# Moving the second branch's gate projection into the attention task stream, with SiLU made of exp, ln and exp

## The chip, the cores and the metric

The kernel runs on the 8 cores of one Trainium2 chip. Each core takes one of the 8 sequences of the batch and does all four layers on it; the cores exchange nothing. The metric is the device time of the slowest core in microseconds (us).

## What is computed

Each layer normalises its input, projects it once to 9216 columns, and runs two mixers on the projection. Cut to what matters here:

```
h = rmsnorm(x, g_norm[layer]);  proj = h @ w_in[layer]
a_u, a_v, a_gate, q, k, v, b_gate, gate_logits = jnp.split(proj, splits, axis=-1)
y_a = chunked_spatial_gating(gelu(a_u), gelu(a_v), ...) * silu(a_gate)
y_b = dilated_attention(q, k, v) * silu(b_gate)
g_a, g_b = jnp.split(sigmoid(gate_logits), N_BRANCHES, axis=-1)
merged = g_a * (y_a @ w_proj_a[layer]) + g_b * (y_b @ w_proj_b[layer])
x = x + merged @ w_out[layer]
```

A core has 2048 positions and a model width of 1024. The attention has 16 heads of 64 channels and three patterns: keys at distance up to 128 in steps of 1, up to 512 in steps of 4, up to 2048 in steps of 16. The three share one softmax denominator. The part at issue is `silu(b_gate)`: a 1024 by 1024 projection of `h`, x / (1 + exp(-x)) of it, and the product with the attention's output.

## The kernel before, in words

**Layout.** Activations lie transposed, channels on the 128 partitions. `HT` holds the normalised input, `VY` the output of a branch, `M` the merged result, each as 8 channel tiles of 2048 positions in bf16; `XT` is the residual in f32. Since all of them are views of one allocation, the profile calls every SBUF tile "arena" and every PSUM bank "ps". A projection is made of items: one item is 8 matmuls of 128x128 weights against 512 positions into one of the 8 PSUM banks.

**Order.** The program is written as one list per engine (`Prog`). An instruction waits for what it depends on and for nothing else, but each engine runs its list in order, so the order in which the code emits decides what queues behind what. Only TensorE does not wait for its own earlier instructions by semaphore; ScalarE and VectorE do.

**Stages of a layer.** In this order: the V projection with a round trip through a DRAM buffer `vd` (from which keys' values are gathered by stride), the first q and k projections, the attention, the B gate (lines 573 to 586), the merge with `w_pb` (`proj_merge`, L588), the branch A stages, the merge with `w_pa`, and the output projection with the next layer's normalisation.

**Attention.** The heads go in 8 pairs (`hp`). A pair has 4 blocks of 512 queries, and a block has 10 score tasks: 8 of the first two patterns (`s_fn`, L489) and 2 of the third (`s3_fn`, L516; 16 matmuls of 32 columns). A score task computes scores into one bank, ScalarE takes exp of the bank into a `PT` tile, VectorE multiplies it with the mask. Its `pv` function later multiplies the tile with the values, into the block's output banks 0 to 3. For pairs 0 to 6, 8 items of the next pair's q and k projection (`qk_item`, L430) are put between the tasks, one after every fifth; pair 7 has none. After a block's last product, `norm_fn` (L537) takes ln of both denominators and exp of the negative on ScalarE, and two VectorE products write the normalised output to `VY`. At a pair's start `gen_masks` (L458) makes the pair's masks by 6 exps on ScalarE.

**The emission loop (L558 to L571)** walks over all tasks of a layer. At step t it emits task t's score part and then the product part of task t-3:

```
tk["sb"] = 4 + t % 4
tk["pt"] = PT[t % 5]
```

So the score banks 4 to 7 are used in turn by every task, q and k items included, and a task's bank is wanted again four steps later.

**Weights.** `chunks` (L257) lists all weight blocks of 1024x256 in the order of use. Four slots of SBUF hold them; `w_release` issues the DMA for the next block on the POOL queue, and the block waits there until the slot's readers are through. The values are loaded from `vd` on the SP queue by `load_v0` (double buffered), `load_v1` and `load_v2` (single buffers, so each is loaded when the pair before has used it for the last time).

**The B gate stage** runs after the last attention task. It takes 32 items through `proj_fm` (L343); each ends in a Silu on ScalarE (L582) and one VectorE product into `VY` (L583).

Of the kernel before, what the change touches and what calls it, by code (L numbers as in the profile page):

```python
# [174 lines left out]
def build(l0, l1, final):  # L175
# [18 lines left out]
    P = Prog(nc)  # L194
# [63 lines left out]
    for l in range(l0, l1):  # L258
# [3 lines left out]
        for j in range(4):  # L262
            chunks.append(cw(3072, j))
            chunks.append(cw(4096, j))
        for j in range(4):
            chunks.append(cw(6144, j))
        for j in range(4):
            chunks.append(w_pb[l, :, j * WCOLS:(j + 1) * WCOLS])
# [23 lines left out]
    def w_acquire():  # L292
        i = wstate["next_use"]
        wstate["next_use"] = i + 1
        return WS_[i % NSLOT]
# [77 lines left out]
    for l in range(l0, l1):  # L373
# [43 lines left out]
        def load_v1(hp):  # L417
            rk = tuple(("vd", hp, i_) for i_ in range(16))
            P.dma("sp", "vl1", lambda e: e.dma_start(
                out=VL1.ap.rearrange("p (r b) c -> p r b c", r=4),  # L420
                in_=vd[:, hp, :].rearrange("(b p r) c -> p r b c", b=4, p=128, r=4)), reads=rk, writes=VL1.k())
# [8 lines left out]
        def qk_item(hp, which, s, qb=7):  # L430
# [10 lines left out]
            if (hp % 2 == 1) and which == 1 and s == 3:  # L441
                w_release()
                w_release()

        items = [(w, s) for s in range(4) for w in range(2)]
        for ii, (w, s) in enumerate(items):
            qk_item(0, w, s, ii)
# [6 lines left out]
        for hp in range(8):  # L454
# [94 lines left out]
            if hp + 1 < 8:  # L549
                for ii, (w_, s_) in reversed(list(enumerate(items))):  # L550
                    ptasks.insert(5 * ii + 5, dict(
                        s=lambda tk, hp=hp, w_=w_, s_=s_: qk_item(hp + 1, w_, s_, tk["sb"]),
                        pv=lambda tk: None, before=[], after=[]))
                ptasks[9]["after"].append(lambda hp=hp: load_v0(hp + 1))
                ptasks[-1]["after"].append(lambda hp=hp: load_v1(hp + 1))
            tasks += ptasks

        SKEW = 3  # L558
# [12 lines left out]
                    f()  # L571

        ti = [0]
        for j in range(4):
            wsl = w_acquire()
            for f2 in range(2):
                hp = 2 * j + f2

                def ev(s, bank, hp=hp):
                    t1 = T1[ti[0] % 4]  # L580
                    ti[0] += 1
                    act(t1.ap, PS[bank][:, :], AF.Silu, psk(bank), t1.k())  # L582
                    tt(VY.ap[:, hp, s * 512:(s + 1) * 512], VY.ap[:, hp, s * 512:(s + 1) * 512], t1.ap, ALU.mult,  # L583
                       VY.k2(hp, s * 512, (s + 1) * 512) + t1.k(), VY.k2(hp, s * 512, (s + 1) * 512))
                proj_fm(wsl, f2 * 128, next_banks(), ev)
            w_release()

        def proj_merge(accumulate):  # L588
            for j in range(4):
# [235 lines left out]
```

How the kernel before makes its waits and increments, by code:

```python
            def run(e, eng):  # L111
                for ins in self.ins[e]:
                    for src, val in ins["waits"]:
                        v = cnts[src[1]][val] if src[0] == "e" else val
                        eng.wait_ge(sems[src], v)
                    r = ins["fn"](eng)
                    if ins["dma"] is not None:
                        r.then_inc(sems[("d", ins["dma"])], 16)
                    elif ins["signal"]:
                        r.then_inc(sems[("e", e)], 1)
                if e == "sp":
                    for g in final_waits:
                        eng.wait_ge(sems[("d", g)], self.groups[g])
```

## Time and profile before

| | |
|---|---|
| median of the 2 runs shown | 4704.23 us (4436.76 and 4971.7) |
| time of the profiled execution | 4439.41 us |
| span of its slowest core, core 2 | 4437.8 us |
| spans of the other cores | 4403.8 to 4431.1 us |
| TensorE busy | 4182.8 us, 94% of the span, 31168 matmuls |
| VectorE busy | 1815.1 us, 41% |
| ScalarE busy | 1746.9 us, 39% |
| chain of waits that ended last | TensorE 86%, ScalarE 5%, DMA 5%, issue 2%, VectorE 2% |
| ScalarE table loads | 29, of 1283 ns |
| mean granted TensorE clock of the core | 0.940 |

Times in the profile are us from the start of the span of core 2 unless marked ns. PE is TensorE's matmuls, PEld its weight loads, DVE is VectorE, ACT is ScalarE, POOL and SP are the queues that issue DMAs. L241, L246, L252 and L255 are the lines of the helpers for a matmul, an activation, a product or sum of two tensors, and a copy. The granted clock is 1.00 at 2.4 GHz and 0.50 at 1.2 GHz; a mean between the two is a stretch that had both.

### The profile page before, as it was taken

The page shows a single profiled execution, that of the slowest core. Times are in us where ns is not written, and L with a number is a line of the kernel's source. Part 1 is how long each engine was busy: PE and PEld are TensorE (multiplying, and loading weights), DVE is VectorE, ACT ScalarE, POOL GpSimd, SP SyncE. Part 2 cuts the span into 40 slices and gives each one's busy share as a digit, 9 for nine tenths or more (in the row PEclk, how much of TensorE's full clock was granted, in tenths as well). Part 3 has the DMA queues.
Part 4 walks back from the last instruction along what each step waited for, and adds up shares of the span by engine and source line. Part 5 has one row for each costly group of instructions (what it writes and reads, how often), then busy time and mean ns, then how long its engine had stood idle before and what let it go on. Part 6 is the DMA issues. An engine that isn't in the chain of part 4 may idle for free.

```text
span 4437.8 us, 84096 instructions; the slowest of 8 cores (4403.8 to 4437.8 us)
## 1 busy us (share of the span) xinstructions
PE 4182.8 (94%) x31168; PEld 2447.0 (55%) x31168; DVE 1815.1 (41%) x3285; ACT 1746.9 (39%) x3085; POOL 170.3 (4%) x200
## 2 busy tenths in 40 slices
PE   5999999899899999999989999999999999999997
PEld 3666654644566665554466666464446666646444
DVE  3344432353444442244434444224443444323435
ACT  3355541421245553242225555233222555524213
POOL 0000000000000000000000000000000000000000
PEclk7999979999999988999999997999999999799999
DMA  4522212322342221222252221223224222122222
GB/s 123 106 52 53 51 27 34 43 34 39 70 86 54 54 47 20 39 39 38 29 111 53 54 53 40 29 29 48 39 34 110 54 54 54 30 34 38 34 34 86
DMA packets 426842, 227.99 MB, mean 51 GB/s; under 512 B 204368, under 2 KB 421840, under 8 KB 426448
## 3 DMA queue, kind: packets, MB, share of 16 engines
q0 software_dynamic: 199808, 100.68, 18.0%
q1 hardware_dynamic: 226640, 121.93, 9.6%
q8 instruction: 262, 4.29, 0.4%
q14 instruction: 132, 1.08, 0.1%
HBM read 289.71 MB, written 33.55 MB: 73 GB/s over the span
## 4 chain that ended last, share of the span: by engine, by line
PE 86%; ACT 5%; DMA 5%; issue 2%; DVE 2%; ACTq 0%; DVEq 0%; SPq 0%; POOL 0%; POOLq 0%
PE ps L241 85%; ACT arena L246 5%; DMA arena<-vd 2%; DVE arena L252 1%; DMA arena<-w_in 1%; DMA arena<-x 1%; DVE arena L356 0%; PE ps L317 0%; DMA out<-arena 0%; PE ps L759 0%; PE ps L383 0%; DVE arena L338 0%; DVE arena L255 0%; DVE arena L361 0%; ACTq L115 0%
## 5 line engine op out<-in xcount | busy, mean ns | idle before, releaser
L241 PE MATMUL ps<-arena 128*128 128x512 bf16 (+5 forms) x30880 | 4134.3, 297 | 182.8 <-DVE arena L252 70.6
L241 PEld LDWEIGHTS ps<-arena 128*128 128x128 bf16 (+1 forms) x30880 | 2407.5, 111 | 1908.7 <-issue 591.0
L246 ACT ACTIVATE arena<-ps 128x512 bf16<-128x512 f32 (+2 forms) x2400 | 1388.8, 595 | 2352.0 <-PE ps L241 2054.2
L252 DVE TENSOR_TENSOR arena<-arena 128x512 bf16<-128x512 bf16 (+1 forms) x1600 | 710.4, 457 | 895.8 <-ACT arena L246 869.2
L252 DVE TENSOR_TENSOR arena<-ps,arena 128x512 bf16<-128x512 f32 (+3 forms) x800 | 529.1, 673 | 1059.9 <-PE ps L241 816.6
L255 DVE CAST arena<-ps 128x512 bf16<-128x512 f32 x320 | 221.4, 692 | 388.8 <-PE ps L241 385.5
L246 ACT ACTIVATE arena<-arena 128x512 bf16<-128x512 f32 (+4 forms) x528 | 262.9, 528 | 249.5 <-DVE arena L252 105.1
L289 POOL DMA_DIRECT2D arena<-w_in x144 | 126.3, 878 | 3009.0 <-PE ps L241 2991.8
L697 DVE SCALAR_TENSOR_TENSOR arena<-arena,ps 128x512 bf16<-128x512 bf16 x128 | 88.1, 688 | 92.0 <-ACT arena L246 92.0
L356 DVE SCALAR_TENSOR_TENSOR arena<-arena 128x512 bf16<-128x512 f32 x128 | 86.2, 746 | 28.6 <-ACT arena L246 28.6
L700 DVE SCALAR_TENSOR_TENSOR arena<-arena 128x512 bf16<-128x512 bf16 x128 | 88.6, 692 | 13.7 <-DVE arena L697 0.5
L248 ACT ACTIVATE arena<-arena 128x1024 bf16<-128x1024 f32 x64 | 67.7, 1057 | 6.1
L246 ACT ACT_TABLE_LOAD x29 | 37.2, 1283 | 73.9 <-PE ps L241 49.0
L317 PE MATMUL ps<-arena 128*128 128x128 f32 x128 | 24.0, 343 | 25.3 <-DMA arena<-x 22.2
L338 DVE TENSOR_SCALAR arena<-ps 128x512 f32<-128x512 f32 x20 | 13.8, 692 | 71.4 <-PE ps L241 71.4
L255 DVE COPY arena<-ps 128x512 f32<-128x512 f32 x32 | 22.0, 691 | 42.7 <-PE ps L317 36.8
L383 PE MATMUL ps<-arena 128*128 128x128 f32 x32 | 9.9, 401 | 28.9 <-DVE arena L252 27.5
L317 PEld LDWEIGHTS ps<-arena 128*128 128x128 f32 x128 | 18.7, 177 | 30.2 <-issue 30.1
L289 POOL DMA_DIRECT2D arena<-w_pb x16 | 14.0, 874 | 545.7 <-PE ps L241 545.7
L655 DVE TENSOR_SCALAR arena<-arena 128x1024 bf16<-128x1024 bf16 x64 | 28.6, 483 | 11.4 <-ACT arena L246 8.0
L289 POOL DMA_DIRECT2D arena<-w_pa x16 | 14.0, 873 | 400.6 <-PE ps L241 400.6
L361 DVE SCALAR_TENSOR_TENSOR arena<-arena 128x512 f32<-128x512 f32 x32 | 21.6, 746 | 7.8 <-ACT arena L246 7.8
(14 smaller groups left out, 72.8 us busy)
## 6 DMA issues: line engine op xcount, KB each, us to landing
arena<-w_in POOLq DMA_DIRECT2D x144, 512.0 KB, 7.0
arena<-vd SPq DMA_DIRECT2D x96, 768.0 KB, 7.2
vd<-arena SPq DMA_DIRECT2D x128, 192.0 KB, 1.9
arena<-x SPq DMA_DIRECT2D x16, 512.0 KB, 14.3
arena<-w_pb POOLq DMA_DIRECT2D x16, 512.0 KB, 5.9
arena<-w_pa POOLq DMA_DIRECT2D x16, 512.0 KB, 5.8
arena<-w_o POOLq DMA_DIRECT2D x16, 512.0 KB, 7.0
out<-arena SPq DMA_DIRECT2D x16, 512.0 KB, 7.8
```

The lines of the kernel that those rows point to most:

```text
L241: P.op("pe", lambda e: e.matmul(out, lhsT=lhsT, rhs=rhs, start=start, stop=stop, skip_group_check=True), reads, writes)
L246: P.op("act", lambda e: e.activation(out=out, in_=in_, func=func, scale=scale), reads, writes)
L248: P.op("act", lambda e: e.activation(out=out, in_=in_, func=func, scale=scale, accum_out=accum_out), reads, writes)
L252: P.op(eng, lambda e: e.tensor_tensor(out=out, in0=in0, in1=in1, op=op), reads, writes)
L255: P.op(eng, lambda e: e.tensor_copy(out=out, in_=in_), reads, writes)
L289: P.dma("pool", "w%d" % (i % NSLOT), lambda e: e.dma_start(out=slot.ap, in_=src), reads=(), writes=slot.k())
L317: P.op("pe", lambda e, bank=bank, c4=c4, xs=xs, ct=ct: e.transpose(PS[bank][:, c4 * 128:(c4 + 1) * 128], xs.ap[:, ct * 128:(ct + 1) * 128] ...
L356: P.op("dve", lambda e, ct=ct, rs=rs: e.scalar_tensor_tensor(out=HT.ap[:, ct, s * 512:(s + 1) * 512], in0=XT.ap[:, ct, s * 512:(s + 1) * 512],
L361: P.op("dve", lambda e, ct=ct, rs=rs: e.scalar_tensor_tensor(out=XT.ap[:, ct, s * 512:(s + 1) * 512], in0=XT.ap[:, ct, s * 512:(s + 1) * 512],
L655: P.op("dve", lambda e, c=c: e.tensor_scalar(out=VN[:, :, c, :], in0=VN[:, :, c, :], scalar1=SSQ.ap[:, c:c + 1], scalar2=None, op0=ALU.mul ...
L697: P.op("dve", lambda e, sgt=sgt, s=s: e.scalar_tensor_tensor(out=sgt.ap, in0=sgt.ap, scalar=1.0, in1=PS[gbk[s]][:, :], op0=ALU.add, op1=AL ...
L700: P.op("dve", lambda e, sgt=sgt, uus=uus: e.scalar_tensor_tensor(out=uus, in0=uus, scalar=0.5, in1=sgt.ap, op0=ALU.mult, op1=ALU.mult), uu ...
```

## The change

It drops the B gate stage. Its 32 items become `bg_item`s: those of pairs 0 to 6 are tasks in the attention stream of the pair that follows, 4 in each of the pairs 1 to 7, at place 3 of each quarter of the pair's task list; the 4 of pair 7 come after the stream, in banks 0 to 3. Silu is replaced by exp, ln(1 + .), exp(- .), so sigmoid comes out, and a VectorE product with the bank. The gate weights move forward in `chunks`: each j now has its q, k and gate block in a row.

```diff
         for j in range(4):
             chunks.append(cw(3072, j))
             chunks.append(cw(4096, j))
-        for j in range(4):
             chunks.append(cw(6144, j))
...
+        bg_slots = {}
+
+        def bg_item(p, sp_, qb, tl):
+            j = p // 2
+            if j not in bg_slots:
+                bg_slots[j] = w_acquire()
+            wsl = bg_slots[j]
+            c0 = (p % 2) * 128
+            for ct in range(8):
+                mm(PS[qb][:, :], wsl.ap[:, ct, c0:c0 + 128], HT.ap[:, ct, sp_ * 512:(sp_ + 1) * 512],
+                   ct == 0, ct == 7, wsl.k2(ct) + HT.k2(ct, sp_ * 512, (sp_ + 1) * 512), psk(qb))
+            act(tl.ap, PS[qb][:, :], AF.Exp, psk(qb), tl.k(), scale=-1.0)
+            P.op("act", lambda e: e.activation(out=tl.ap, in_=tl.ap, func=AF.Ln, bias=1.0), tl.k(), tl.k())
+            act(tl.ap, tl.ap, AF.Exp, tl.k(), tl.k(), scale=-1.0)
+            tt(tl.ap, PS[qb][:, :], tl.ap, ALU.mult, psk(qb) + tl.k(), tl.k())
+            yk = VY.k2(p, sp_ * 512, (sp_ + 1) * 512)
+            tt(VY.ap[:, p, sp_ * 512:(sp_ + 1) * 512], VY.ap[:, p, sp_ * 512:(sp_ + 1) * 512], tl.ap, ALU.mult,
+               yk + tl.k(), yk)
+            if (p % 2 == 1) and sp_ == 3:
+                w_release()
...
+            if hp >= 1:
+                per = len(ptasks) // 4
+                for b_ in reversed(range(4)):
+                    ptasks.insert(per * b_ + 3, dict(
+                        s=lambda tk, hp=hp, b_=b_: bg_item(hp - 1, b_, tk["sb"], tk["pt"]),
+                        pv=lambda tk: None, before=[], after=[]))
...
-        for j in range(4):
-            wsl = w_acquire()
-            for f2 in range(2):
-                hp = 2 * j + f2
-
-                def ev(s, bank, hp=hp):
-                    t1 = T1[ti[0] % 4]
-                    ti[0] += 1
-                    act(t1.ap, PS[bank][:, :], AF.Silu, psk(bank), t1.k())
-                    tt(VY.ap[:, hp, s * 512:(s + 1) * 512], VY.ap[:, hp, s * 512:(s + 1) * 512], t1.ap, ALU.mult,
-                       VY.k2(hp, s * 512, (s + 1) * 512) + t1.k(), VY.k2(hp, s * 512, (s + 1) * 512))
-                proj_fm(wsl, f2 * 128, next_banks(), ev)
-            w_release()
+        for s_ in range(4):
+            bg_item(7, s_, s_, T1[s_])
```

## Rows read from the trace of the kernel before

**Rows 1.** Windows: length, busy (count) by engine, clock, DMA; layer 0's attention, gate
```profile
162.10:609.30 447.20, 420.80 (x4386) 279.40 (x4386) 212.80 (x439) 247.84 (x456) 7.00 (x8) 0.90 0.24 52
609.30:664.60 55.30, 55.30 (x259) 25.09 (x257) 14.57 (x33) 20.97 (x35) 2.62 (x3) 1.00 0.23 29
```

**Rows 2.** Windows of the B gate stage of all four layers, the sum
```profile
sum 221.50, PE 221.50 PEld 100.37 DVE 58.25 ACT 84.15 POOL 10.48; mean PE 55.38 PEld 25.09 DVE 14.56 ACT 21.04 POOL 2.62
```

**Rows 3.** Windows of layer 0's attention: pair 1, pair 4, and pairs 1 to 6
```profile
215.50:273.20 57.70, 52.94 (x558) 34.76 (x557) 27.30 (x57) 31.84 (x61) 0.87 (x1) 0.94 0.25 56
385.80:438.40 52.60, 50.56 (x558) 33.49 (x558) 27.37 (x57) 30.63 (x56) 0.87 (x1) 1.00 0.23 50
215.50:551.30 335.80, 314.88 (x3338) 206.70 (x3338) 163.97 (x337) 187.60 (x349) 5.24 (x6) 0.95 0.25 53
```

**Rows 4.** Windows of pair 7: layer 0, a stretch inside it, four layers' sum
```profile
551.30:609.30 58.00, 54.87 (x502) 39.26 (x502) 22.38 (x49) 31.40 (x56) 0.89 (x1) 0.56 0.17 32
...
561.00:605.00 44.00, 43.74 (x400) 30.70 (x401) 16.55 (x36) 22.79 (x39) 0.00 (x0) 0.50 0.01 1
...
sum 231.40, PE 219.51 PEld 157.10 DVE 89.57 ACT 124.74 POOL 3.51; mean PE 54.88 PEld 39.27 DVE 22.39 ACT 31.18 POOL 0.88
```

**Rows 5.** TensorE's waits (us, times, longest): layer 0's attention, then layer 3's
```profile
PE ps L241 <- DVE arena L252: 18.9, 30, 2.0
PE ps L241 <- DMA arena<-vd: 7.0, 4, 2.8
...
PE ps L241 <- DVE arena L252: 17.4, 31, 2.0
PE ps L241 <- DMA arena<-vd: 0.9, 1, 0.9
```

**Rows 6.** TensorE's waits in layer 0: pairs 1 to 6, then pair 7
```profile
PE ps L241 <- DVE arena L252: 15.1, 25, 2.0
PE ps L241 <- DMA arena<-vd: 5.8, 3, 2.8
...
PE ps L241 <- DVE arena L252: 1.9, 1, 1.9
PE ps L241 <- DMA arena<-vd: 1.2, 1, 1.2
```

**Rows 7.** Timeline (start, length, engine, line) around one block's end, layer 0, pair 2
```profile
286.44 2.55 ACT L246 ACTIVATE arena<-ps 128x512 bf16<-128x512 f32 x4 [2.05 <-PE ps L241]
...
289.08 0.63 ACT L246 ACTIVATE arena<-arena 128x512 f32<-128x512 f32 x1
289.62 1.55 ACT L246 ACTIVATE arena<-ps 128x512 bf16<-128x512 f32 x3
289.88 1.48 DVE L252 TENSOR_TENSOR arena<-ps,arena 64x512 bf16<-64x512 f32 x2 [1.66 <-ACT arena L246]
291.38 1.10 DVE L252 TENSOR_TENSOR arena<-arena 128x512 bf16<-128x512 bf16 x3
...
291.95 0.72 PE L241 MATMUL ps<-arena 128*128 128x128 bf16 x6 [0.53 <-DVE arena L252]
```

**Rows 8.** Groups (busy, mean ns, idle before) in layer 0's B gate stage
```profile
L246 ACT ACTIVATE arena<-ps 128x512 bf16<-128x512 f32 x31 | 18.4, 597 | 32.8 <-PE ps L241 32.8
L252 DVE TENSOR_TENSOR arena<-arena 128x512 bf16<-128x512 bf16 x31 | 13.2, 425 | 38.6 <-ACT arena L246 38.6
```

**Rows 9.** Timeline of TensorE at the start of pair 7, layer 0
```profile
550.73 4.63 PE L241 MATMUL ps<-arena 128*128 128x128 bf16 x50
557.30 2.77 PE L241 MATMUL ps<-arena 128*128 128x128 bf16 x30 [1.95 <-DVE arena L252]
561.26 2.08 PE L241 MATMUL ps<-arena 128*128 128x128 bf16 x19 [1.19 <-DMA arena<-vd]
```

**Rows 10.** Timeline of ScalarE, layer 0: the first table load since the attention began
```profile
611.35 1.28 ACT L246 ACT_TABLE_LOAD   x1 [0.40 <-PE ps L241]
```

**Rows 11.** The page's DMA issues: count, size, median us to landing
```profile
arena<-vd SPq DMA_DIRECT2D x96, 768.0 KB, 7.2
```

## The prediction

> **What bounds the kernel now.** I read the table of engines and the chain of waits first: TensorE is busy in 94% of the span and carries 86% of the chain, so what counts is what happens to TensorE's time. The windows by stage come next. The B gate stage of a layer is 55.3 us in which TensorE is never idle and the clock is 1.00 [rows 1]; in four layers it is 221.5 us [rows 2]. The attention is 447.2 us in layer 0, of which TensorE is idle for 26.4, at a mean clock of 0.90 [rows 1]. So the stage that goes away has no slack in it, and the one that takes its work in has two kinds: idle time of TensorE, and time at the lower clock.
>
> Idle time: TensorE waits 18.9 us for VectorE and 7.0 us for the values' DMA in layer 0's attention, 17.4 and 0.9 in layer 3's [rows 5]; pairs 1 to 6 of layer 0 have 15.1 and 5.8 of it [rows 6]. Clock: pair 4, all of it at 1.00, takes 52.6 us, pair 1, at 0.94, takes 57.7 [rows 3]. Pair 7 has no q and k items, yet takes 58.0 us at 0.56, and 44 us of it lie wholly at 0.50, the 1.2 GHz level [rows 4]. The timeline shows what came before the fall: an idle 1.95 us behind the masks' VectorE work and 1.19 us for the values' DMA, within 6 us [rows 9]. The clock then stays low through narrow matmuls of 32 and 128 columns, and is back as soon as the gate stage's 512-column matmuls begin (1.00 in the second of rows 1).
>
> **What an item costs on TensorE.** The gate stage is 32 items in 55.3 us, 1.73 us each [rows 1]. All 128 are still done. If nothing else happened, the change would move 221.5 us and save nothing: the gain must come from slack.
>
> **Gate stage out, tail in.** Out go 55.4 us per layer [rows 2]. Four items remain after the stream: 6.9 us. The last two use banks 2 and 3, which the last block's normalisation still reads: in [rows 7] that takes from about 287.7 (two of the four in the first row are its ln) to 291.36, 3.7 us, and the first two items cover 3.5. I take 7.3 us. The merge does not wait for them: its product matmuls for a block of positions need only that block's item, and those for the last block come seven groups of 8 matmuls, 12 us, after the last item, against about 3 us of chain behind it. The Silu table load falls away (1.28 us [rows 10]); it ran on ScalarE while TensorE worked, so it is worth nothing. Exp and Ln alternate all through the attention with no table load before that one [rows 10], so the new ln adds none.
>
> **24 items in pairs 1 to 6.** They add 24 x 1.73 = 41.5 us of TensorE work. Does their ScalarE and VectorE work make TensorE wait? An item needs exp from the bank 0.60 [rows 8], ln and exp in SBUF about 0.63 each (the row of 0.63 [rows 7]), then a product with the bank at about 0.74 (half of the 1.48 [rows 7]) and one in SBUF at 0.43 [rows 8]. The old stage had one of 0.60 and one of 0.43. On average there is room: pair 4 has ScalarE busy 30.6 of 52.6 us and VectorE 27.4 [rows 3]; with four items each they come to 38 and 32 of about 59.
>
> But the items land at the worst place, just behind a block's normalisation. I walk through it from the end of the last block's products (287.5). Now: ScalarE does ln, ln, exp until 289.7, then three exps back to back until 291.2; VectorE's two normalising products end at 291.36, the mask product behind them at 291.8, and TensorE starts at 291.95 after 0.53 idle [rows 7]. With the item two tasks after the block's start: TensorE has 1.73 us more to do, ScalarE does the next task's exp until 290.2 and then the item's three until 292.2, and the exps of the two tasks behind it end at about 292.7 and 293.2. VectorE frees the item's bank near 293.1, finishes the item near 293.6, and has the next two masks at 294.0 and 294.5. On TensorE the item, three tasks' matmuls and a q or k item lie ahead of the task that wants the bank: it gets there at about 294.1, and to the first of these masks at 294.5. Nothing waits, and the old 0.53 us is gone, since the item lies in front of it. So in these pairs the item covers most of the waits for VectorE. It covers most of the DMA waits too, because it stands between the issue of `load_v1` and its first use: with 1.73 us more in between, a wait of at most 2.8 us [rows 6] is at most 1.1.
>
> Of the 20.9 us of idle in pairs 1 to 6 of layer 0 [rows 6], less in layer 3 (18.3 in all pairs [rows 5]), I take 18.5 as the mean and let 80% go: -15. The weight loads shift: three instead of two come near the end of pairs 2, 4 and 6, on the POOL queue, where each waits for its slot's readers only. Every block is issued ten tasks or more ahead of its use, and nothing but weights is queued behind it there. Their cost is that they share the DMA engines with the values' loads (7.2 us to landing [rows 11]); at worst the DMA waits double, +5.8, at best nothing.
>
> **The clock.** Price of the lower level: pair 4 without its 8 items is 52.6 - 13.8 = 38.8 us at 1.00; pair 7, the same tasks, is 58.0 at 0.56. So 19.2 us for 88% of 58 us at the low level, 0.38 us per us. Pairs 1 to 6 have a mean of 0.95 [rows 3], 33 us at 0.50 per layer, worth 12.6 us. The lower level follows idle stretches there, and these shrink; I let half of it come back: -6. Pairs 1 to 6 then add 41.5 - 15 - 6 = 20.5 us. Bounds: 41.5 - 18.5 - 12.6 = 10.4, and, with no slack filled and 0.6 us of new wait per item (one ScalarE instruction), 56.
>
> **Pair 7.** The first of its items stands ahead of both waits of [rows 9], so the clock should not fall there. Warm throughout, it would be 38.8 + 6.9 = 45.7 us. Between its items it has ten tasks and no q or k item, so there ScalarE's chain is not covered as above: the bank is wanted some 0.8 us too early in each block, +3 against some 2 saved. I take it that the clock falls in about a third of the pair, +6, and get 53: -5 against 58. Bounds: warm -11; cold as now, with 6.9 us of items that at 0.50 take twice as long, +12 after the waits they cover.
>
> **Sum per layer:** -55.4 + 7.3 + 20.5 - 5 = -32.6 us, 130 in four layers. Against the profiled execution's 4439.4 that is **4309 us**. That execution is at the level of the lower of the two runs shown (4436.8), not at their median of 4704; the forecast is for executions like it. All at the good end: -55.4 + 7.3 + 10.4 - 11 = -48.7, 4245 us. All at the bad: -55.4 + 7.3 + 56 + 12 = +20, 4519 us.
>
> **Rivals.**
> *Clock stays low in pair 7.* The items come every ten tasks; after each the narrow matmuls return, and [rows 4] show that these alone never brought the clock back in 44 us. Then pair 7 costs +12 instead of -5: 4309 + 4 x 17 = 4377, -1.4%. Against it: in pairs 1 to 6 the same tasks hold a mean of 0.95 with one wide item per five. The Trainium skill, page "TensorE: Matmul & The Clock Gate", section "A second HAM failure mode: psum-queue depth-cycling", speaks for this rival: cycling through PSUM banks lets TensorE idle briefly between groups, often enough that the clock swings between its levels. These tasks cycle through four banks; taken for pair 7 alone the rule gives this rival's time, and its row, 0.56, agrees. Chance 0.17.
>
> *All slack is filled.* Pairs 1 to 7 at 1.00 and without waits: 4245. For it: pair 4 holds 1.00 already. Chance 0.15.
>
> *Slower: the item's chain holds its score bank.* Place: ScalarE, three instructions in a row that wait for each other, and behind them the exps of the next tasks. Price: 0.60 + 0.63 + 0.63 + 0.74 and about 0.25 of semaphores, 2.85 us per item, all of it idle on TensorE for 112 items, with no slack filled: 4439 - 4 x 48.1 + 112 x 1.73 + 319 = 4760. It decides from about 2 us of new wait per item, (130 + 89) / 112; that is 4528. For it: ScalarE already runs without a break through 4.7 us here [rows 7]. Against it: 4.5 us of TensorE work lie between the item and the next user of its bank. Chance 0.07.
>
> **Chances and range.** The forecast's own case has 0.61, with 4270 to 4350 about it. About 2% (89 us) is what a measurement tells from no change, so faster means under 4350: 0.15 of the full gain and 0.55 of the forecast's case, 0.70. Within 2%: the clock rival and the forecast's slow edge, 0.22. Slower: 0.08. The range runs from a little below the full gain to a little above the clock rival with doubled DMA waits (4377 + 4 x 5.8 = 4400): 4235 to 4425.
>
> **What would show it.** Right: after the last attention task only some 7 us of 512-column matmuls before the merge; pairs 1 to 6 at some 356 us in layer 0, waits for VectorE near 3 us; pair 7 near 53 us with a clock of 0.75 or more; 25 table loads. Wrong: waits of TensorE for VectorE of over 1 us right after the items; pair 7 at a clock near 0.6; table loads inside the attention; longer waits for the values' DMA at the starts of pairs 3, 5 and 7.

## The result and the profile after

The changed kernel takes 0.9927 of the time before, interval 0.9910 to 0.9943: some 32 us less, where 130 were forecast. The interval lies clear of 1, but the change is below the 2% that the prediction had called the least that a measurement tells from none. Its executions took 4401.6 to 4415.8 us beside 4436.8 to 4441.2 of the kernel before; the one profiled took 4407.62, against 4439.41. (The higher of the two times shown before, 4971.7, is of a disturbed execution, as some of either kernel are; they are left out.)

The page of the changed kernel: span, busy time of the engines, the chain that ended last, table loads, the values' DMA.

```profile
span 4406.0 us, 84976 instructions; the slowest of 8 cores (4366.7 to 4406.0 us)
...
PE 4190.4 (95%) x31168; PEld 2446.8 (56%) x31168; DVE 1899.9 (43%) x3413; ACT 1886.8 (43%) x3337; POOL 170.3 (4%) x200
...
PE 79%; ACT 8%; DMA 5%; issue 4%; DVE 4%; SPq 0%; ACTq 0%; DVEq 0%; POOL 0%; POOLq 0%
...
L246 ACT ACT_TABLE_LOAD x25 | 32.1, 1283 | 66.5 <-PE ps L241 43.2
...
arena<-vd SPq DMA_DIRECT2D x96, 768.0 KB, 7.9
```

ScalarE and VectorE have more to do, and ScalarE has 8% of the chain where it had 5; TensorE's busy time is hardly changed (4182.8 before), and its busy share is a point higher. What is to be explained is busy time, not waits. The windows of core 2 (the first line of before, the others of after), columns as in [rows 1]: the sum of pairs 1 to 6 over four layers before; then layer 0's pairs 1 to 6, their sum over four layers, pair 1 alone, pair 7 of layer 0 and its sum, the sum of the four items that come behind the stream.

```profile
sum 1335.10, PE 1261.11 PEld 825.18 DVE 656.16 ACT 750.18 POOL 20.98; mean PE 315.28 PEld 206.30 DVE 164.04 ACT 187.55 POOL 5.25
...
213.90:578.40 364.50, 356.74 (x3530) 226.01 (x3529) 190.46 (x385) 228.78 (x421) 7.87 (x9) 0.99 0.26 53
...
sum 1461.80, PE 1433.34 PEld 906.94 DVE 761.18 ACT 915.60 POOL 31.49; mean PE 358.33 PEld 226.73 DVE 190.30 ACT 228.90 POOL 7.87
...
213.90:273.70 59.80, 58.65 (x590) 37.40 (x590) 31.76 (x65) 38.12 (x71) 0.87 (x1) 1.00 0.24 53
...
578.40:645.30 66.90, 63.68 (x533) 41.68 (x533) 26.41 (x57) 37.86 (x68) 0.87 (x1) 0.64 0.16 31
...
sum 262.50, PE 247.36 PEld 162.26 DVE 105.52 ACT 151.33 POOL 3.49; mean PE 61.84 PEld 40.56 DVE 26.38 ACT 37.83 POOL 0.87
...
sum 27.80, PE 27.80 PEld 12.77 DVE 12.60 ACT 24.05 POOL 0.00; mean PE 6.95 PEld 3.19 DVE 3.15 ACT 6.01 POOL 0.00
```

Per layer, the mean of four on core 2, the answer to [rows 1 to 4]:

| part | forecast | measured | from |
|---|---|---|---|
| gate stage out, four items behind the stream | -48.1 | -48.4 | (27.80 - 221.50) / 4 |
| pairs 1 to 6 | +20.5 | +31.7 | (1461.80 - 1335.10) / 4 |
| pair 7 | -5 | +7.8 | (262.50 - 231.40) / 4 |
| rest of the layer | 0 | about +1 | what is left of the sum |
| sum | -32.6 | -8 | 32 us in four layers |

TensorE's waits in layer 0 (us, times, longest), first pairs 1 to 6, then pair 7, against [rows 6]:

```profile
PE ps L241 <- DVE arena L252: 5.6, 22, 0.6
PE ps L241 <- DMA arena<-vd: 1.8, 2, 1.1
...
PE ps L241 <- DVE arena L252: 2.0, 3, 1.4
PE ps L241 <- ACT arena L246: 0.8, 2, 0.6
```

In pairs 1 to 6 the waits fell by 13.5 us, from 20.9 to 7.4, and the clock rose from 0.95 to 0.99. Both slacks that the forecast counted on were used. Yet pair 1 at a full clock takes 59.8 us, and pair 4 of before, at a full clock too, took 52.6 [rows 3]: 7.2 us more for 6.9 us of items. TensorE's busy time alone rose by more, from 50.56 to 58.65 us, 8.1 for 6.9. Something new ate what the waits gave.

**Where it went** shows around the block's end of [rows 7]. First TensorE before, then after, each from its own timeline (start, length):

```profile
287.45 0.41 PE L241 MATMUL ps<-arena 64*128 64x128 bf16 x8
```
```profile
289.01 0.33 PE L241 MATMUL ps<-arena 64*128 64x128 bf16 x3
...
291.33 0.39 PE L241 MATMUL ps<-arena 64*128 64x128 bf16 x4
...
288.95 4.26 PE L241 MATMUL ps<-arena 64*128 64x128 bf16 x40
293.73 4.49 PE L241 MATMUL ps<-arena 128*128 128x128 bf16 x44 [0.51 <-DVE arena L252]
```

The four score matmuls of one task use 64 rows of the array: head 0's operands lie on partitions 0 to 63, head 1's on 64 to 127. The q or k item has no product part, so three steps after it no product stands between the scores of two tasks. These are a task of head 0 and one of head 1, and before the change their eight matmuls took 0.41 us together. Afterwards the new item and a product stand between them: four in 0.39 us, and four more in about as much, 2.3 us later. The Trainium skill, page "TensorE: Matmul & The Clock Gate", section "Part 3: Packing small matmuls — row/col tiling", says that matmuls on different row groups of the array run concurrently. The trace agrees, with eight in 0.41 us beside four in 0.39.

Taken over all the fully warm stretches of pairs 1 to 6 as medians from start to start (my own matching of the matmul records to the order of emission), the two score steps behind a block's normalisation went from 122 and 218 ns to 327 and 327: +0.31 us. The step of the third pattern behind them went from 1.17 to 1.39, +0.22, which is a wait; the 0.51 in the last row above is one of these, a long one. The q or k item that had covered the normalisation went from 2.37 to 1.82, -0.55. The two losses together eat the gain, and the item's own 1.74 us come on top.

The wait is there because the product follows its score at a distance of three *steps*, and an item is a step. The rows of ScalarE and VectorE for this stretch, same columns:

```profile
290.86 0.63 ACT L246 ACTIVATE arena<-arena 128x512 f32<-128x512 f32 x1
291.39 1.06 ACT L246 ACTIVATE arena<-ps 128x512 bf16<-128x512 f32 x2
292.55 0.63 ACT L456 ACTIVATE arena<-arena 128x512 bf16<-128x512 bf16 x1
293.27 0.63 ACT L246 ACTIVATE arena<-arena 128x512 bf16<-128x512 bf16 x1
```
```profile
291.66 1.48 DVE L252 TENSOR_TENSOR arena<-ps,arena 64x512 bf16<-64x512 f32 x2 [1.66 <-ACT arena L246]
293.15 0.43 DVE L252 TENSOR_TENSOR arena<-arena 128x512 bf16<-128x512 bf16 x1
294.01 0.69 DVE L252 TENSOR_TENSOR arena<-ps,arena 128x512 bf16<-128x512 f32 x1 [0.42 <-ACT arena L246]
```

VectorE ends the two normalising products at 293.14, and the mask product that TensorE waits for at 293.58. Before the change, the three steps between the block's third score and its product were the fourth score task, the third pattern's and the q or k item, and the product stood behind that item. Now they are the new item, the fourth task and the third pattern's, and the q or k item comes behind the product. So TensorE has one item and two tasks in between, as before: the new item stands in the other's place and adds no distance.

### The profile page after: what moved, and what is told of

Its sections match the earlier page's. It is cut to its first block, busy times and chain, and to the rows that moved or that the text cites. A ratio compares the mean times of both kernels' runs of the same rounds, so it can differ in the third digit from the quotient of the medians.

```text
span 4406.0 us, 84976 instructions; the slowest of 8 cores (4366.7 to 4406.0 us)
## 1 busy us (share of the span) xinstructions
PE 4190.4 (95%) x31168; PEld 2446.8 (56%) x31168; DVE 1899.9 (43%) x3413; ACT 1886.8 (43%) x3337; POOL 170.3 (4%) x200
## 4 chain that ended last, share of the span: by engine, by line
PE 79%; ACT 8%; DMA 5%; issue 4%; DVE 4%; SPq 0%; ACTq 0%; DVEq 0%; POOL 0%; POOLq 0%
PE ps L241 78%; ACT arena L246 8%; DVE arena L252 3%; DMA arena<-vd 2%; DMA arena<-w_in 1%; DMA arena<-x 1%; DVE arena L355 0%; DMA arena<-w_o 0%; ACTq L115 0%; PE ps L774 0%; DVEq L115 0%; DMA out<-arena 0%; SPq L424 0%; PE ps L382 0%; DVE arena L337 0%
## 5 line engine op out<-in xcount | busy, mean ns | idle before, releaser
L252 DVE TENSOR_TENSOR arena<-ps,arena 128x512 bf16<-128x512 f32 (+3 forms) x928 | 618.0, 676 | 1140.7 <-PE ps L241 829.5
L246 ACT ACTIVATE arena<-arena 128x512 bf16<-128x512 f32 (+4 forms) x656 | 343.7, 548 | 267.8 <-DVE arena L252 104.9
L456 ACT ACTIVATE arena<-arena 128x512 bf16<-128x512 bf16 x128 | 80.8, 631 | 12.6 <-ACT arena L246 1.1
L316 PE MATMUL ps<-arena 128*128 128x128 f32 x128 | 23.8, 342 | 23.9 <-DMA arena<-x 22.7
L337 DVE TENSOR_SCALAR arena<-ps 128x512 f32<-128x512 f32 x20 | 13.8, 692 | 70.5 <-PE ps L241 70.5
L316 PEld LDWEIGHTS ps<-arena 128*128 128x128 f32 x128 | 18.5, 176 | 28.9 <-issue 28.7
```

Source lines behind the costliest of these rows:

```text
L246: P.op("act", lambda e: e.activation(out=out, in_=in_, func=func, scale=scale), reads, writes)
L252: P.op(eng, lambda e: e.tensor_tensor(out=out, in0=in0, in1=in1, op=op), reads, writes)
L316: P.op("pe", lambda e, bank=bank, c4=c4, xs=xs, ct=ct: e.transpose(PS[bank][:, c4 * 128:(c4 + 1) * 128], xs.ap[:, ct * 128:(ct + 1) * 128] ...
L456: P.op("act", lambda e: e.activation(out=tl.ap, in_=tl.ap, func=AF.Ln, bias=1.0), tl.k(), tl.k())
```

## The experiments

All ratios are to the kernel before, with their intervals; where there is none, times of executions stand beside those of the kernels named. The table gives the mean of four layers on core 1, for which the records could be matched to the emitted matmuls one by one in every kernel: time, TensorE's idle time, clock. Core 1 is a little shorter than core 2 (before: 331.6 against 333.8 us in pairs 1 to 6).

| kernel | ratio | pairs 1 to 6 | pair 7 |
|---|---|---|---|
| before | 1 | 331.6, 18.1, 0.96 | 57.4, 2.7, 0.54 |
| after | 0.9927 | 362.8, 6.5, 0.99 | 63.3, 2.7, 0.71 |
| e1_place4 | 0.9862 | 360.3, 23.8, 0.98 | 62.3, 3.6, 0.73 |
| e5_one_act | 0.9852 | 362.1, 5.9, 0.99 | 56.2, 1.1, 0.79 |
| e6_place4_one_act | 0.9826 | 360.2, 24.0, 0.98 | 54.0, 3.1, 0.85 |
| e11_skew4 | - | 358.0, 1.1, 0.96 | 67.1, 5.6, 0.69 |
| e8_eight_in_7 | - | 354.9, 21.8, 0.98 | 68.7, 5.8, 0.84 |
| e4_eight_in_7 | 1.0083 | 354.9, 7.1, 0.99 | 68.2, 5.1, 0.84 |
| e2_wide7 | 0.9989 | 331.6, 17.9, 0.96 | 57.4, 4.0, 0.96 |
| e3_head_order | 1.0236 | 347.5, 15.8, 0.94 | 60.3, 4.9, 0.55 |
| e7_head_pairs | 0.9528 | 295.3, 8.1, 0.93 | 43.6, 5.1, 0.76 |
| e9_pairs_gate | - | 342.8, 16.8, 0.96 | 60.8, 12.5, 0.78 |
| e13_pairs_gate2 | 0.9779 | 356.9, 23.1, 0.92 | 60.9, 13.3, 0.78 |
| e14, the same, one act | 0.9672 | 346.5, 19.9, 0.95 | 56.2, 11.3, 0.81 |
| e10_pairs_eight_in_7 | - | 336.7, 15.1, 0.95 | 59.6, 6.8, 0.89 |
| e12_pairs_only_7 | - | 296.4, 8.1, 0.93 | 61.1, 6.8, 0.86 |
| e15_pairs_wide7 | 0.957 | 297.3, 7.2, 0.92 | 48.2, 1.8, 0.96 |

### The item one place later

```diff
-                    ptasks.insert(per * b_ + 3, dict(
+                    ptasks.insert(per * b_ + 4, dict(
```

> The changed kernel with each moved item one place later (place 4 of its quarter instead of 3), nothing else. Theory P (overlap of two heads): where a q or k item leaves a hole in the products, two score tasks follow each other on TensorE, one on partitions 0 to 63 and one on 64 to 127, and run at the same time (the start-to-start step of the first is 122 ns in the kernel before, 327 ns in the changed one, where the item stands between the two). One place later the item leaves these two together and gives another two the same chance: 0.3 to 0.6 us less per item in pairs 1 to 6, 96 items, so 30 to 58 us below the changed kernel, about 4350 to 4375. Theory C (ScalarE's chain of three): the item is only one task further from the normalisation; at most the 0.23 us of wait at the third-pattern task goes, 0 to 22 us less, 4385 to 4408.

Measured: 0.9862 [0.9814, 0.9909]. The two score steps behind the normalisation are back at 122 and some 220 ns, and a second such pair has come up (224 and 356), since the new item has no product part either. But the steps behind them grew, the third pattern's to 1.81 us and another to 0.68. In layer 0 the waits of pairs 1 to 6 show it; the second row is one of these waits.

```profile
PE ps L241 <- DVE arena L252: 20.2, 39, 1.0
...
298.16 4.07 PE L241 MATMUL ps<-arena 128*128 128x128 bf16 x48 [0.92 <-DVE arena L252]
```

So the overlap is real and one place away, and it is largely traded for waits: 17.3 us more idle time per layer than after, yet 2.5 us less in all (table). The executions took 4377.8 to 4397.1 us, on average 19 under the changed kernel's, where the overlap theory had 30 to 58.

### Two of the three ScalarE operations left out

```diff
-            P.op("act", lambda e: e.activation(out=tl.ap, in_=tl.ap, func=AF.Ln, bias=1.0), tl.k(), tl.k())
-            act(tl.ap, tl.ap, AF.Exp, tl.k(), tl.k(), scale=-1.0)
```

> The changed kernel with the item's ln and second exp left out (one ScalarE instruction per item instead of three; the gate's values are then not sigmoid). Theory C (the chain of three is what ate the gain): without it the wait of 0.23 us at the third-pattern task goes in 96 blocks, 21 us, and the waits of pair 7 shrink: 20 to 45 us below the changed kernel, 4362 to 4387. If the broken overlap of two heads is the larger part (theory P), the steps of 327 ns behind the block's start stay as they are and the kernel stays above 4360. If the chain were all of it, the kernel would come near my forecast of 4309.

> Place 4 and one ScalarE instruction per item (ln and second exp left out). In the place-4 kernel the overlaps are back (122 and 224 ns), but the step of the third-pattern task has grown from 1170 to 1814 ns and one score step from 356 to 678. Theory C+P (both costs are real, and place 4 trades one for the other): both steps go back, 0.9 us in 96 blocks, 70 to 100 us below the place-4 kernel, 4290 to 4320. Rival (these steps wait for TensorE's own order, not for ScalarE): no change from 4388.

Measured: e5, at place 3, 0.9852 [0.9837, 0.9867]; e6, at place 4, 0.9826 [0.9804, 0.9847]. In pairs 1 to 6 nothing moved: 362.1 beside 362.8, and 360.2 beside 360.3; the third pattern's step stays at 1.39 and 1.81 us. So the waits there do not come from the item's ScalarE chain, which is what e6 was to find out; what is left is the normalisation, whose ScalarE and VectorE work stands ahead of the mask product, as in the rows above (read from the rows; no run changed that order). The forecast for e6 (some 70 to 100 us under place 4) was missed by far; it came out about 20 under it. All of the gain lies in pair 7. There four layers of e5 read, on core 2:

```profile
sum 230.10, PE 220.64 PEld 149.31 DVE 106.56 ACT 132.64 POOL 3.50; mean PE 55.16 PEld 37.33 DVE 26.64 ACT 33.16 POOL 0.87
```

That is 57.5 us per layer against 65.6 after: the chain costs 8.1 us per layer in pair 7 (7.1 on core 1) and nothing in pairs 1 to 6. Only 1.4 us of the 8.1 are idle time of TensorE (3.8 against 2.4 us); 6.7 are busy time, and go with a clock of 0.68 against 0.78. In pair 7 no q or k item stands beside the chain.

### A distance of four steps

```diff
-        SKEW = 3
+        SKEW = 4
```

> The changed kernel with the product part four steps behind the score part instead of three, nothing else. Theory S (the wait behind the normalisation was never covered by the item, because the distance between a score task and its product is counted in steps, and the item takes one of them): one more step is 0.7 to 1.7 us more for every mask, the waits at the third-pattern task (0.23 us in 96 blocks) and most of pair 7's (3.8 us per layer) go, 20 to 50 us below the changed kernel, 4355 to 4385. Rival (those waits come from an engine that is simply full): within 10 us of 4406.

Measured: 4382.1 to 4394.8 us, 18 under the changed kernel on average, where 20 to 50 were expected. The waits for VectorE in layer 0's pairs 1 to 6 are gone (0.2 us in one wait, beside 5.6), but the pairs fell by 4.8 us only, with the clock at 0.96 instead of 0.99, and pair 7 got longer (67.1), with twice the idle time (5.6). So the distance in steps was what left the wait: a pair that is at the full clock throughout takes 57.4 us where it takes 59.4 in the changed kernel. Why the clock is lower is open.

### What the overlap is worth

The kernel before, all tasks of head 0 in a block ahead of those of head 1:

```diff
-                for wi in range(0, 8, 2):
-                    for hh in range(2):
+                for hh in range(2):
+                    for wi in range(0, 8, 2):
```

> The kernel before, with the score tasks of a block ordered all of the first head, then all of the second, so that neighbours use the same half of the partitions. Theory P (overlap of two heads): the quick steps of 122 and 218 ns become about 330 each, 0.3 us per hole and two holes per block, 0.6 us for 28 x 4 blocks and less where a wait covers it: the kernel is 30 to 75 us slower than before. Rival (the quick steps come from weight loads that ran ahead during the wait before them): nothing changes, within 10 us.

The kernel before, with the scores of two heads issued together and the two products behind them; the q and k items moved between such pairs of tasks:

```diff
+            n = 2 if (t + 1 < len(tasks) and tasks[t].get("head") == 0
+                      and tasks[t + 1].get("head") == 1) else 1
+            for u in range(t, t + n):
...
+                    tk["s"](tk)
+            for u in range(t, t + n):
...
+                    tk["pv"](tk)
...
-                    ptasks.insert(5 * ii + 5, dict(
+                    ptasks.insert(10 * (ii // 2) + (4, 10)[ii % 2], dict(
```

> The kernel before, where the two heads' score tasks of the same work are emitted one right after the other, then the two products; the q and k items stand between such pairs and the two third-pattern tasks are neighbours. Theory P: eight more pairs of score tasks per head pair overlap, 0.31 us each, and four pairs of third-pattern tasks, some 0.5 us each: 4 to 5 us per head pair, 32 of them, less what turns into waits for ScalarE: 50 to 150 us faster than before. Rival (the overlap needs the preceding wait, which lets the queue fill): within 15 us of before.

Measured: e3 is slower, 1.0236 [1.0193, 1.028]. It is +105 us, where 30 to 75 were expected. With the same head on both sides of the missing product the eight matmuls no longer run side by side: by medians as above, the eight score steps of a full block of the first two patterns take 3.38 us instead of 2.71, 0.34 us per q or k item, which would be 76 us over 224 items. The rest goes with a lower clock (0.94 against 0.96 in pairs 1 to 6 on core 1) and a pair 7 that is 2.9 us longer though it has no such item; why is open. e7, which lets every pair of tasks overlap, is the fastest kernel of this study: **0.9528 [0.9512, 0.9543]**, 4230 to 4240 us. It has the B gate stage as before. Its page (span and engines), layer 0's pairs 1 to 6, and pair 7's sum:

```profile
span 4238.1 us, 84320 instructions; the slowest of 8 cores (4205.6 to 4238.1 us)
...
PE 4008.5 (95%) x31168; PEld 2402.0 (57%) x31168; DVE 1803.7 (43%) x3285; ACT 1727.1 (41%) x3085; POOL 170.3 (4%) x200
...
210.70:514.70 304.00, 291.17 (x3339) 203.10 (x3340) 161.93 (x337) 184.93 (x349) 5.24 (x6) 0.92 0.28 59
...
sum 176.90, PE 154.76 PEld 124.78 DVE 87.39 ACT 114.54 POOL 3.50; mean PE 38.69 PEld 31.20 DVE 21.85 ACT 28.64 POOL 0.88
```

TensorE's busy time fell by 174 us with the same 31168 matmuls. "95% busy" had hidden an array with half of its rows unused.

### The studied change on top of it

e9 and e13 put the gate items into e7's stream, between pairs of tasks; e9 at attention place 8 of each block, e13 with the first of a pair at place 2. In e9, and in e10 further down, the gate, q and k blocks are used in another order than they were loaded in, so they are exchanged; the work is the same. In e13 and e14 they are used in the order of loading. e14 leaves ln and the second exp out. The cut is e13's; e9 has `10 * b_ + 8` for every block.

```diff
+                    more.append((10 * b_ + 8 if b_ else 2, dict(
+                        s=lambda tk, hp=hp, b_=b_: bg_item(hp - 1, b_, tk["sb"], tk["pt"]),
```

> The head-pair kernel (4238) with the studied change on top: the gate items with exp, ln, exp in the stream, one per block in pairs 1 to 7, each between two pairs of score tasks and away from the normalisation. If the idle and the low clock that an item can fill are what the change is worth, and no overlap of heads is broken: the stage of 55.4 goes, each item costs 1.73 us less what it fills; pairs 1 to 6 have 1.6 us of idle and a clock of 0.92 in the head-pair kernel, so 1.5 to 3 us each come back, 10 to 18 per layer, and pair 7 0 to 5: 4165 to 4200. If the chain of three costs TensorE more in this denser stream (theory C): 4220 to 4260.

> The head-pair kernel with the studied change on top, the first gate item of a pair ahead of its first q item so that gate, q and k weight blocks are used in the order of loading; items at places 2, 18, 28 and 38 of the 40 tasks, each between two pairs of tasks. If overlaps kept are all that was missing: 1.5 to 3 us per pair of idle and low clock come back, 4165 to 4205. If the chain of three ScalarE instructions costs as much here as in pair 7 of the run with two items per block there: 4235 to 4280, no better than the head-pair kernel's 4238.

> The same with the item's ln and second exp left out. Theory C: 25 to 60 us below the run before, near 4200. If the chain is covered in pairs 1 to 6 and costs in pair 7 alone: 10 to 30 us below.

Measured: e9 4278.8 to 4282.9 us; e13 0.9779 [0.9748, 0.981], 4334 to 4346 us; e14 0.9672 [0.963, 0.9714], 4279 to 4293. Both e9 and e13 had been expected at 4165 to 4205 by the theory I favoured, at 4220 to 4280 by the other, and are above both. They are slower than e7 without the change, e9 by some 48 us, e13 by about 107. Layer 0 of e13, pairs 1 to 6, and TensorE's waits there:

```profile
210.00:570.70 360.70, 336.81 (x3531) 220.18 (x3531) 183.37 (x383) 224.44 (x414) 7.87 (x9) 0.92 0.25 51
```
```profile
PE ps L241 <- ACT arena L246: 10.6, 6, 2.3
...
PE ps L241 <- DMA arena<-vd: 7.3, 2, 4.2
...
PE ps L241 <- DVE arena L252: 4.7, 17, 0.5
```

Against e7 on core 1, 41.5 us of items cost 61.6 in pairs 1 to 6, and 6.9 cost 17.3 in pair 7: +31 us per layer after the 48 that the stage gives back (by the ratios 111 us in all). Most of it is idle time, 15.0 us more in pairs 1 to 6 and 8.2 in pair 7 (table). In pairs 1 to 6 of all four layers (core 2) the waits for ScalarE all come in a pair's first block, behind the item at place 2. In layer 0's pair 2, ScalarE has the pair's six mask exps there (first row), then exps of scores, the normalisation's, the item's three; TensorE waits for it at the third pattern's task (second row).

```profile
267.28 2.14 ACT L246 ACTIVATE arena<-arena 128x256 bf16<-128x256 f32 x6 [1.11 <-DVE arena L252]
```
```profile
275.38 0.82 PE L241 MATMUL ps<-arena 64*128 64x32 bf16 x10 [2.26 <-ACT arena L246]
```

e14, without two thirds of the chain, is 10.4 us per layer shorter in pairs 1 to 6 and 4.7 in pair 7, some 50 us in all. But e9 has the full chain and is a little faster still. It differs from e13 in one place per pair, 8 instead of 2 (and by it in the exchanged blocks), and in layer 0's pairs 1 to 6 it has no wait for ScalarE:

```profile
PE ps L241 <- DVE arena L252: 13.7, 13, 2.2
PE ps L241 <- DMA arena<-vd: 3.6, 2, 1.9
```

So on this order the chain costs pairs 1 to 6 time where the item stands beside the mask exps, not everywhere, and neither the better place nor a shorter chain brings the change down to e7; the two together were not tried. In the odd pairs of e13 and e14 stand 24 us of waits for the values' DMA (four layers, core 2); e7 has 15 of them already. The weights' DMA adds 5.5 us there in e13 and 11.2 in e14. The cause of what was added is open.

### Pair 7: clock, chain or items

e2 is the kernel before, with eight items in pair 7 whose result nobody uses (8 matmuls of 512 columns each, no evictions). e15 is the same on e7. Both do that work in addition.

```diff
+                def wide(tk):
+                    for ct in range(8):
+                        mm(PS[tk["sb"]][:, :], WS_[0].ap[:, ct, 0:128], HT.ap[:, ct, 0:512], ...)
```

> The kernel before, with 8 useless items of 8 matmuls of 512 columns put into pair 7, one after every fifth task, their results unread. Theory W (pair 7 is slow for want of wide matmuls: the clock falls at its start and narrow matmuls do not bring it back): pair 7 takes about 52 to 55 us instead of 58 although it does 13.8 us more, with a clock over 0.9; the kernel is 12 to 24 us faster than before. Rival (the clock follows the waits, not the kind of matmul): pair 7 stays near 0.56 and takes at least 58 + 13.8 us; the kernel is 55 us or more slower.

> The head-pair kernel with 8 useless items of 8 wide matmuls in pair 7, no ScalarE or VectorE work with them. The same kernel with 8 true items there had pair 7 at 61.9 us with a clock of 0.86 and 7.9 us of idle. If the chain is what holds pair 7: 49 to 52 us, clock over 0.93, idle under 3 us, though the kernel as a whole is then 20 to 32 us slower than the head-pair kernel (the work is extra). If it is the clock's own behaviour between sparse items: above 58 us.

e4 and e8 keep four gate items in each of the pairs 1 to 5 and put the last eight into pair 7. e8 has them where the q and k items would be and the others at place 4; e4 has them two tasks earlier (`5 * ii + 3`), not behind every fifth task as its expectation says, and issues three weight loads per layer too few, so that blocks come late and are not the right ones. The cut is e8's. e10 is the same on e7's order. e12 is e7 with eight true gate items in pair 7 and 24 left in the stage.

```diff
+            if hp == 7:
+                for ii in reversed(range(8)):
+                    ptasks.insert(5 * ii + 5, dict(
+                        s=lambda tk, ii=ii: bg_item(5 + ii // 4, ii % 4, tk["sb"], tk["pt"]),
```

> The changed kernel with pair 7 hosting 8 items (those of pairs 5 and 6) after every fifth task, and pair 6 none; pairs 1 to 5 as in the changed kernel. Theory W (wide matmuls hold the clock of pair 7): pair 7 takes 53 to 56 us with 8 items where it now takes 65.6 with 4, its clock is over 0.9, pair 6 goes back to about 53.5 from 61; in all 60 to 85 us below the changed kernel, 4320 to 4345. Rival (waits at the start of the pair hold the clock down): pair 7 near 72 us and no gain over the changed kernel beyond 5 us.

> Items of pairs 5 and 6 in pair 7 (8, after every fifth task), none in pair 6, the others at place 4. The useless-item run had pair 7 at 57.5 us with a clock of 0.94 (57.8 and 0.55 before). Theory W: pair 7 at 58 to 62 us with a clock over 0.85, pair 6 at about 54; 25 to 45 us below the place-4 kernel. Theory C: eight chains of three in 57 us make TensorE wait for ScalarE and the clock falls again, pair 7 at 66 us or more and nothing gained over place 4.

> As the run before, but pair 7 hosts 8 items (of pairs 5 and 6) and pair 6 none. Pair 7 of the place-4 kernel with 8 such items took 68.7 us with waits for the chain, the one with 8 useless items 57.5 us. With the heads in pairs I expect 54 to 58 us for pair 7 if the chain costs little, 60 or more if it is what holds it; in all within 25 us of the run before, faster if the clock counts more, slower if the chain does.

> The head-pair kernel with only pair 7 hosting items: 8 of them (pairs 0 and 1), with exp, ln, exp; the other 24 stay in the stage of their own with Silu. Pair 7 has 44.3 us at a clock of 0.78 and 6.2 us of idle without items. Theory W: it comes to 50 to 54 us with 8 items of 1.73 us, so 4 to 8 us per layer are gained, 4205 to 4222. Theory C: the chain makes it 58 us or more, nothing gained or a loss, 4235 to 4255.

Measured: e2 0.9989 [0.9964, 1.0013]; e15 0.957 [0.9542, 0.9598]; e4 1.0083 [1.0049, 1.0117]; e8 4381.6 and 4388.3 us; e10 4258 to 4269; e12 4245.0 and 4247.2. Of these, e8 came out level with place 4 (4377.8 to 4397.1) and e12 at 4235 to 4255, both as the chain theory had it; e10 is some 17 us under e9. e4 had been expected 60 to 85 us under the changed kernel and is some 78 above it: not by the attention, which is no longer (table), but by waits for weights, 131 us on core 1 against 37. I had expected e2 to win 12 to 24 us. It wins nothing, and loses nothing with 13.8 us of useless work in each pair 7. Pair 7's sums over four layers on core 2, first e2, then e15, then e12:

```profile
sum 230.60, PE 215.68 PEld 142.44 DVE 88.96 ACT 119.37 POOL 3.50; mean PE 53.92 PEld 35.61 DVE 22.24 ACT 29.84 POOL 0.88
```
```profile
sum 193.80, PE 187.18 PEld 132.44 DVE 90.39 ACT 117.46 POOL 3.50; mean PE 46.80 PEld 33.11 DVE 22.60 ACT 29.37 POOL 0.88
```
```profile
sum 244.20, PE 216.71 PEld 148.78 DVE 115.84 ACT 168.48 POOL 5.80; mean PE 54.18 PEld 37.20 DVE 28.96 ACT 42.12 POOL 1.45
```

Three things follow. **The price of the clock:** before, pair 7 took 57.85 us at 0.55; e2 has 57.65 at 0.94 and 13.8 us of it are the added items. So e2 does the same tasks in 57.65 - 13.8 = 43.85 us, 14.0 less. Not all of that is the clock's. A useless item has no product part either, so twice in a block two tasks of different heads come to run side by side in e2, which they never do in pair 7 of before:

```profile
567.41 0.41 PE L241 MATMUL ps<-arena 64*128 64x128 bf16 x8
```

With 0.31 us or more for each of the seven full ones, that is at least 2 us (an estimate), and leaves some 11 to 12 for the low clock, not the 19.2 of the prediction. That had taken pair 4 without its items as its measure, which has the side-by-side tasks that pair 7 lacks, and is among the shortest pairs; pair 1 takes over 5 us more [rows 3]. **The items hold the clock** with no evictions behind them: 0.94 and 0.96, from the same four banks in turn. **The chain:** e12 and e15 differ in pair 7 by the evictions of eight items per layer (and in which weights these read), and in 61.05 - 48.45 = 12.6 us, 1.6 us per item: 5.2 of it idle time of TensorE and 7.4 busy time, at 0.86 against 0.96. In e12's first pair 7 TensorE waits for ScalarE; ScalarE's rows, then TensorE's:

```profile
523.15 0.60 ACT L246 ACTIVATE arena<-ps 128x512 bf16<-128x512 f32 x1 [2.26 <-PE ps L241]
523.84 0.63 ACT L457 ACTIVATE arena<-arena 128x512 bf16<-128x512 bf16 x1
524.56 0.63 ACT L246 ACTIVATE arena<-arena 128x512 bf16<-128x512 bf16 x1
525.10 2.37 ACT L246 ACTIVATE arena<-ps 128x512 bf16<-128x512 f32 x4
```
```profile
526.24 0.38 PE L241 MATMUL ps<-arena 64*128 64x128 bf16 x4 [1.81 <-ACT arena L246]
```

From 523.15 to 525.10 ScalarE works on one item alone, and the score banks of the tasks behind it wait for their exp.

## Why the prediction was wrong

The number was wrong: a quarter of the forecast gain came, and not by either faster case. The steps one by one.

**Gate stage out, tail in: right.** -48.4 against -48.1; the tail has TensorE busy for all of its 6.95 us, and 25 table loads are left, none of them in the attention.

**24 items in pairs 1 to 6: most of the slack came, and a term was missing.** By the sums of core 2, TensorE's idle time there went from (1335.10 - 1261.11) / 4 = 18.5 us to (1461.80 - 1433.34) / 4 = 7.1: 11.4 us, where the forecast had 15. The step that failed is "Nothing waits, and the old 0.53 us is gone, since the item lies in front of it". I had counted the item's 1.73 us as work that comes between a score and its product. It takes one of the three steps and sends the q or k item behind the product, so a wait is there again, 0.51 us in the row shown, 0.22 in the median; e11, with a fourth step, takes it away. That is 3.6 us per layer.

The larger part is a term that the sum did not have. I had taken TensorE's other durations as given, while the item parts two tasks that had run side by side: 0.31 us. Over 24 items that is 7.4 us, and the busy time shows it: it rose by (1433.34 - 1261.11) / 4 = 43.1 us, where the forecast has 41.5 - 6 = 35.5. What is left of it agrees with the 6 us that were taken for the clock. So 3.6 + 7.6 = 11.2 us per layer, the whole miss of these pairs, 45 us in four layers. e3 and e7 show what the overlap is worth, from both sides (+2.4%, -4.7%, though e3 has more in it). e1 gives it back, with a second pair of tasks on top, and comes out only 9 us (core 1 of the profiled executions) to 29 us (by the ratios) below, since waits for VectorE come up in its place.

**Pair 7: the mechanism was half right, the size wrong.** The chain that is not covered there had been put at "+3 against some 2 saved", and measures 8.1 us (e5), of which only 1.4 are waiting, as the +3 was meant, and the rest goes with the lower clock. "I take it that the clock falls in about a third of the pair" measures a mean clock of 0.64 to 0.71, thus more than half of it. The price per us was too high besides (11 to 12 us where it has 19.2). At the start of layer 0's pair 7 the DVE waits are 0.27, 0.37 and 1.39 us:

```profile
578.14 6.01 PE L241 MATMUL ps<-arena 128*128 128x128 bf16 x53
584.42 0.71 PE L241 MATMUL ps<-arena 128*128 128x128 bf16 x6 [0.27 <-DVE arena L252]
...
586.47 2.22 PE L241 MATMUL ps<-arena 128*128 128x128 bf16 x24 [0.37 <-DVE arena L252]
590.08 2.31 PE L241 MATMUL ps<-arena 128*128 128x128 bf16 x20 [1.39 <-DVE arena L252]
```

The waits of [rows 9] are shorter and did not go away: the forecast had said that the first item stands ahead of both. +7.8 instead of -5 is 51 us in four layers.

**The rivals.** *Clock stays low in pair 7* gave +12 and 4377 us, and is nearest of the three in pair 7 (+7.8); it did not hold there as stated, for the four items did raise the clock, from 0.55 to 0.68; with eight it stands at 0.84 to 0.86 (e8, e12). The rule of the Trainium skill's page "TensorE: Matmul & The Clock Gate", section "A second HAM failure mode: psum-queue depth-cycling", that cycling through banks lets the clock swing, does not decide here: e2 and e15 cycle through the same four and stand at 0.94 and 0.96. *The item's chain holds its score bank* was right as a mechanism only where no q or k item covers it: pair 7 (1.6 us per item by e12 and e15, of 2.85 at most), and, on e7's order, behind the item that stands beside the mask exps (e13, and not e9).

**Bounds.** Pairs 1 to 6 came within 10.4 to 56 and pair 7 within -11 to +12. The whole came to the upper part of the range (4407 is inside 4235 to 4425), since both misses have one sign.

**Not settled:** the added waits for DMAs in the odd pairs of e13 and e14; the lower clocks of e11 and e3. A version with a shorter chain that still gives the full result was not tried.

## What to carry to other kernels

Before you put work into a stream, look at what stands on both sides of the place: narrow matmuls on different rows may be running side by side, and a busy TensorE does not show it. Compare the time of 8 neighbours with the time of 4. In a stream whose products follow their scores by a number of steps, an inserted item takes a step; count what lies between producer and consumer after the insertion, in microseconds. And where a matmul stage has no waits, moving it can win only the slack of its new place: here changing the order of two heads won 4.7%, moving 221 us of work 0.7%.

## What the runs showed of the hardware

- Eight score matmuls of 64 rows and 128 columns, four on each half of the array, take 0.41 us; four on one half take 0.39 (before and after).
- In pair 7, 13.8 us of useless 512-column matmuls cost no time (57.65 us against 57.85), since the clock goes from 0.55 to 0.94 with them and the tasks behind some of them run side by side. On the faster order, where all do so anyway, they cost 4.25 us: 48.45 against 44.2 of e7, at 0.96 against 0.75.
- Three dependent ScalarE operations of 128x512 hold the engine for 1.95 us (e12): 0.60, 0.63 and 0.63, and under 0.1 between them.
